# Grid attention on tokens ordered by column, with 192 or 256 keys per query tile, and weight splits one unit further ahead

## The reference

```python
def neighbourhood_attn(q, k, v, rpb):
    B, S = q.shape[0], q.shape[1]
    rows = S // GRID_W
    kr = min(NB_ROWS_MAX, rows)
    kc = NB_COLS
    ...
    row_start = jnp.clip(jnp.arange(rows) - kr // 2, 0, rows - kr)
    c_idx = jnp.arange(GRID_W)
    col_start = jnp.clip(c_idx - kc // 2, 0, GRID_W - kc)
    col_nb = col_start[:, None] + jnp.arange(kc)[None, :]
    ...
        s = jnp.einsum('bwhd,brwchd->bhwrc', q_row, k_nb,
                       preferred_element_type=jnp.float32) * scale + bias
        p = jax.nn.softmax(s.reshape(B, B_HEADS, GRID_W, kr * kc), axis=-1)
        p = p.reshape(B, B_HEADS, GRID_W, kr, kc).astype(v_nb.dtype)
        return jnp.einsum('bhwrc,brwchd->bwhd', p, v_nb)
```

```python
        mixed = jnp.einsum('bse,ed->bsd', jnp.concatenate([tok, mem_out], axis=-1), w_out[i])
        x = x + rms_norm(mixed, norm_mix_post[i])
        h = rms_norm(x, norm_ffn_pre[i])
        gu = jnp.einsum('bsd,df->bsf', h, w_gu[i])
        f = jnp.einsum('bsf,fd->bsd', jax.nn.silu(gu[..., :D_FF]) * gu[..., D_FF:], w_down[i])
        x = x + rms_norm(f, norm_ffn_post[i])
```

## Time and profile before

| | |
|---|---|
| runs | 2116.99, 2123.36, 2128.32 us, median 2123.36 |
| profiled execution | 2113.97 us, its span 2112.2 us, TensorE clock granted 0.978 |
| busy | PE 95%, weight loads of PE 77%, DVE 46%, ACT 37%, POOL 8% |
| chain that ended last | PE 89%, ACT 4%, DVE 4%, DMA 2%, issue 1% |
| DMA | 184.44 MB, 87 GB/s in the mean; a 512 KB weight load lands 3.2 to 3.3 us after its issue in the median |

### The profile page before, as it was taken

One profiled execution on the slowest core, in us unless ns is written; L12 is line 12 of the kernel. 1 busy time (PEld: TensorE's weight loads), 2 busy tenths in 40 slices (PEclk: granted clock), 3 DMA queues, 4 the chain that ended last, 5 costly groups with the idle time before them and its releaser, 6 DMA issues.

```text
span 2112.2 us, 24708 instructions
## 1 busy us (share of the span) xinstructions
PE 2013.9 (95%) x10206; PEld 1633.1 (77%) x10206; DVE 970.7 (46%) x1507; ACT 774.5 (37%) x1355; POOL 179.0 (8%) x201
## 2 busy tenths in 40 slices
PE   8899999999999998999999999979899999999997
PEld 6776778888878866778888878957777888888886
DVE  4465554443244286454443235252254455524632
ACT  4376432223232286432223223263363343312221
POOL 3010210000004040120000002000010010000000
PEclk9999999999999999999999999989899999999999
DMA  6620223233324220223223323201102332322232
GB/s 175 157 81 22 74 95 98 92 100 92 100 67 145 90 71 11 70 90 100 92 98 94 101 85 115 90 26 60 48 1 83 103 107 90 100 99 92 98 100 80
DMA packets 53448, 184.44 MB, mean 87 GB/s; under 512 B 6893, under 2 KB 8301, under 8 KB 53209
## 3 DMA queue, kind: packets, MB, share of 16 engines
q1 hardware_dynamic: 49656, 169.17, 24.5%
q0 software_dynamic: 3536, 13.64, 3.2%
q10 hardware_dynamic: 144, 0.06, 0.0%
HBM read 177.60 MB, written 5.24 MB: 87 GB/s over the span
## 4 chain that ended last, share of the span: by engine, by line
PE 89%; ACT 4%; DVE 4%; DMA 2%; issue 1%; POOL 0%; DVEq 0%; SPq 0%; ACTq 0%
PE bank L1162 25%; PE bank L1163 24%; PE bank L1164 24%; PE bank L1267 2%; PE bank L1282 2%; PE bank L1248 2%; PE bank L1188 2%; PE bank L1187 2%; PE bank L1186 2%; DMA w_raw<-in_w_mem_k 1%; DVE prob_short L883 1%; PE bank L1389 1%; PE bank L1422 1%; DVE prob_short L905 1%; ACT pt_short L585 1%
## 5 line engine op out<-in xcount | busy, mean ns | idle before, releaser
L1162 PE MATMUL bank<-h_hi,w_hi 128*128 128x512 f32 x1568 | 624.5, 398 | 40.8 <-DVE w_lo L794 19.9
L794 DVE TENSOR_TENSOR w_lo<-w_raw,w_hi 128x1024 fp32r<-128x1024 f32 (+1 forms) x326 | 404.3, 1242 | 508.7 <-ACT w_hi L491 508.2
L1163 PE MATMUL bank<-h_lo,w_hi 128*128 128x512 f32 x1568 | 617.1, 394 | 0.0
L1164 PE MATMUL bank<-h_hi,w_lo 128*128 128x512 f32 x1568 | 616.8, 393 | 0.0
L491 ACT CAST w_hi<-w_raw 128x1024 fp32r<-128x1024 f32 (+1 forms) x326 | 328.4, 1009 | 365.1 <-DMA w_raw<-in_w_down 77.7
L1162 PEld LDWEIGHTS bank<-h_hi,w_hi 128*128 128x128 f32 x1568 | 298.7, 191 | 114.7 <-issue 37.5
L1163 PEld LDWEIGHTS bank<-h_lo,w_hi 128*128 128x128 f32 x1568 | 299.1, 191 | 63.2 <-issue 1.9
L1164 PEld LDWEIGHTS bank<-h_hi,w_lo 128*128 128x128 f32 x1568 | 298.5, 190 | 63.4
L1162 PE MATMUL bank<-a_hi,w_hi 128*128 128x512 f32 (+1 forms) x752 | 290.5, 386 | 0.9 <-issue 0.9
L1164 PE MATMUL bank<-a_hi,w_lo 128*128 128x512 f32 (+1 forms) x752 | 289.2, 385 | 0.0
L1163 PE MATMUL bank<-a_lo,w_hi 128*128 128x512 f32 (+1 forms) x752 | 289.1, 384 | 0.0
(11 more groups left out here) (178 smaller groups left out, 1878.3 us busy)
## 6 DMA issues: line engine op xcount, KB each, us to landing
w_raw<-in_w_gu SPq DMA_DIRECT2D x88, 512.0 KB, 3.2
w_raw<-in_w_mlp_in SPq DMA_DIRECT2D x32, 512.0 KB, 3.2
w_raw<-in_w_mlp_out SPq DMA_DIRECT2D x32, 512.0 KB, 3.8
w_raw<-in_w_down SPq DMA_DIRECT2D x32, 448.0 KB, 3.3
w_raw<-in_w_out SPq DMA_DIRECT2D x24, 512.0 KB, 3.3
w_raw<-in_w_down SPq DMA_DIRECT2D x16, 512.0 KB, 3.5
w_raw<-in_w_gates SPq DMA_DIRECT2D x16, 512.0 KB, 3.2
w_raw<-in_w_qk_b SPq DMA_DIRECT2D x14, 512.0 KB, 3.3
```

The source lines that it names most:

```text
L794: nc.vector.tensor_tensor(slot(w_lo, v), slot(w_raw, v), slot(w_hi, v).bitcast(F32), ALU.subtract).then_inc(w_split, 1)
L1162: mm(acc, w1, hi, start=start, stop=False)
L1163: mm(acc, w1, lo, start=False, stop=False)
L1164: last = mm(acc, w2, hi, start=False, stop=end)
```

## The change

1. At the turn from layer 0 to layer 1, h is written in another order of tokens: by column of the grid, then row (column 0's 8 tokens, column 1's, and so on). Source and squares follow (by_column, columns_of). All of layer 1's projections and its attention are then in that order; the outputs are put back into the old order as they are copied out of PSUM, for memory heads too. A tile of 128 queries is then 16 whole columns, and its keys are 24, 32, 32 or 24 neighbouring columns: 192, 256, 256 and 192 keys, from key 0, 64, 192 and 320 on. Each step has two blocks of transposes and values a head in place of four.
2. So that key blocks fall on whole tiles of values, values are stored shifted by 64 tokens: each tile is read as two halves of 64 partitions (read_shifted_values).
3. The biases are one table of 128 by 256 a head (2 loads a pair) and a constant of masks (grid_masks, 128 by 640), loaded once by POOL before the phase; three additions a head (192, 192 and 256 columns) make the three tables.
4. Splits go one unit further: hi_to and lo_to to u + 3 in dense and values, to unit 7 at the start, to the eighth unit in leads and behind add_normed.

```diff
             for c in range(6):
-                for i in range(4):
-                    b0 = (6 - 2 * i) * GRID
-                    both = [dict(q=q_buf[rows(half), c, P * i:P * i + P], k=k_buf[rows(half), c, :],
-                                 bias=bias_grid[:, 2 * (c % 2) + half, b0:b0 + S], width=S, keys=S,
+                for i, (k0, keys, b0, blocks, tiles, key_rows) in enumerate(spans):
+                    both = [dict(q=q_buf[rows(half), c, P * i:P * i + P], k=k_buf[rows(half), c, k0:k0 + keys],
+                                 bias=bias_grid[:, 2 * (c % 2) + half, b0:b0 + keys], width=keys, keys=keys,
                                  first_key=0, sink=None, at=0) for half in range(2)]
...
-                hi_to(split + 3)
+                hi_to(split + 4)
...
-                        nc.scalar.copy(o_hi[:, steps[d].pair, :], ps[6 + steps[d].pair_no % 2][:, :]).then_inc(o_hi_done, 1)
+                        dst, src = o_hi[:, steps[d].pair, :], ps[6 + steps[d].pair_no % 2][:, :]
+                        if phase == 1:
+                            dst, src = by_column(dst), columns_of(src)
+                        nc.scalar.copy(dst, src).then_inc(o_hi_done, 1)
...
-            hi_to(6)
+            hi_to(7)
...
+            def read_shifted_values(g, accs):
+                for kt in range(4):
+                    for half in range(2):
+                        tile, to = (kt + half, 1 - half) if 0 < kt + half < 4 else (0, half)
+                        nc.scalar.activation(v_buf[rows(to), tile, 256 * g:256 * g + 256], accs[kt][rows(half), :256],
+                                             ACT.Copy, scale=col[rows(half), kt:kt + 1]).then_inc(acc_read_act, 1)
...
-                        lo_to(u + 2)
+                        lo_to(u + 3)
...
-                    trail(c, xT[:, c, :], h_hi[:, c, :], h_lo[:, c, :], pre)
+                    src, dst_hi, dst_lo = xT[:, c, :], h_hi[:, c, :], h_lo[:, c, :]
+                    if columns_first:
+                        src, dst_hi, dst_lo = by_column(src), columns_of(dst_hi), columns_of(dst_lo)
+                    trail(c, src, dst_hi, dst_lo, pre)
```

127 lines of the change are left out of this document (74 added, 53 removed).

## The result

The changed kernel took 2113.62 us, the median of six runs (2110.09 to 2115.30), beside 2124.47 for the kernel before. The ratio is 0.995 with a 95% interval of 0.9932 to 0.9969, so it is faster by 7 to 14 us. The forecast was 2100 us with a range of 2083 to 2112: direction right, gain of the medians 10.9 us where 23.2 were forecast, and the time just above the range. The profiled execution took 2111.95 us, its span 2110.2; against the profiled one of before that is only 2.0 us of span, and part of the story is why the two profiles say 2 and the medians 11.

What follows compares the result with a forecast made beforehand. The prediction took TensorE (PE) to bound the kernel: its work plus its gaps. Terms -26.1 + 0.7 + 1.6 + 5.6 - 12.0 + 5.6 + 1.4 gave -23.2 us, forecasting a 2100 us median, range 2083 to 2112.

Steps and rivals of the forecast that it cites:

- the one of the values: Layer 1's values before grid attention: reads in halves of 64 partitions lengthen PE's wait, +1.6 us.
- the reads just keep up: 0: Other stages: a unit takes 5.4 us, landing, cast and split 5.5, so splitting further ahead costs 0.
- So 9.1 against 13.45, six pairs: -26.1: Layer 1's grid attention: each head pair takes 9.1 us in place of 13.45, -26.1 us over six pairs.
- The passage: Grid attention: ScalarE's copy and VectorE's subtraction of a head pair, in series on the path, slower by 0.7 us through permuted access.
- the 0.3 for GpSimd's additions: Grid attention: GpSimd's table additions and VectorE's scaling stand in each other's way, 0.3 us a pair.
- the clock falling in the layer turn: Rival, turn of the layers: PE's pauses halve its clock, 1.2 us over the pace in six chunks, 2107 us; chance 0.05.
- So each of eight chunks gives its +0.7 to PE: +5.6: Turn from layer 0 to 1: permuted h_hi and h_lo writes lengthen each chunk by 0.7 us, +5.6 us.
- Four reads took 1.57 us, eight take 3.1: +1.6: Layer 1's values: the last group's reads before grid attention double in number and time, +1.6 us.
- PE goes on near 80.5: +5.6: Start: the memory's statistic waits behind unit 11's late cast, and the bias table copy starts later, +5.6 us.
- Both gaps go: 3.7 + 1.6 + 3.7 + 3.0, -12.0: gate_up, both layers: splitting the eighth unit ahead of the statistic removes PE's stops and the half clock after them, -12.0 us.
- +1.4: Before the window attention: the last read of memory values stands behind a later weight cast, +1.4 us.
- It lies 9.4 below the median: The profiled execution of before, 2113.97 us, against the timed median 2123.36; so 2090.8 became a forecast median of 2100.

Runs made afterwards that it cites:

- no_permute: The changed kernel with copies between the two token orders made in plain order, leaving out the reordering: 2098.02 us, 0.9901 of the kernel before.
- leads_only: The changed kernel with splits one unit further only where a stage is entered, two ahead elsewhere and at the start: 2101.63 us, 0.9917 of the kernel before.
- splits_only: The kernel before with only the splits moved one unit further: 2118.02 us, 1.0002 of the kernel before.
- late_sub: leads_only with VectorE's subtraction for a head pair's low half one step later: 2080.14 us, 0.9823 of the kernel before.
- best2: leads_only plus the late subtraction, the residual's next addition ahead of h_lo and idle matmuls in PE's pauses, table copy in one piece: 2063.99 us, 0.973.
- start_six: The changed kernel with units split only up to 6 at the start: PE goes on at 80.85 us, window attention entered at 125.74 us.

## Why the prediction was wrong, step by step

In the forecast's own terms the step that failed most is the one of the values: PE's wait ahead of the grid attention was priced at +1.6 and the clock behind it at nothing. The wait was 4.01 us for 1.66, the clock fell to half behind it, and grid attention and w_out together came out 3.9 to 5.5 us over the forecast. The second is "the reads just keep up: 0", which cost 3.7 us.

- **"So 9.1 against 13.45, six pairs: -26.1."** Right in its size, 9.08 at full speed, but in part by luck. The passage had 0.81 and not 0.7; the narrow pair without it took 8.27 and not 8.06 (no_permute); and the 0.3 for GpSimd's additions isn't there, since the pair from 796.74 to 805.82, in which GpSimd adds nothing, takes 9.08 as well. The three errors cancel. (Two pairs in 26.97 us are 13.49 each, a difference of 0.2 in the sum.) The attention still lost 3.3 us of its gain and w_out 2.2, by half speed. The forecast had the clock falling in the layer turn, as a rival with 0.05; there the later pauses were 1.2 and 1.6 us and the clock held.
- **"In other stages a unit takes 5.4 us [...] so the reads just keep up: 0."** Wrong: in the gates some units take 1.4 or 2.7 us, and PE waits 1.8 us for a_lo; +3.7. leads_only takes it back whole. Without half speed behind it, in splits_only, it is 2.7. The forecast looked at the mean stage and not at the shortest unit.
- **"So each of eight chunks gives its +0.7 to PE: +5.6."** Mechanism right, size 7.6: h_hi +0.5 and h_lo +0.37 in place of 0.3 and 0.4, in seven periods and in the first pause (5.32 for 4.52).
- **"Four reads took 1.57 us, eight take 3.1: +1.6."** Measured 3.92 and +2.35. Half the partitions is not half the price, nor the same price: 0.49 for 0.39. And the clock behind the longer wait was left out: half speed for up to 12 us of the attention from there, 3.8 us of time when the wait is filled (late_sub against best2).
- **"PE goes on near 80.5: +5.6."** Casts and copy as forecast; 6.7, and 1.2 more through half speed behind the wait. Of its two causes the later copy was worth only 0.7 (start_six).
- **"Both gaps go: 3.7 + 1.6 + 3.7 + 3.0, -12.0."** Right: -5.2 and -6.1.
- **"+1.4" ahead of the window attention.** Right: 1.42.
- **"It lies 9.4 below the median."** The forecast took its own profiled execution as any other and shifted the result. The second one, 11.65 us longer, shows that 9.7 us of that are one attention's half speed, 75.5 or 85.2 us for the same instructions. The shift was harmless for the median, but 6.7 us of the difference between the two profiles, in attentions that the change doesn't touch, mean nothing.

In medians the miss is 13.6 us, 1.1 of it because three more runs raised the median of before. By the stretches it is 2.7 to 3.7 (gates), 2.3 (start), 2.0 and 0.75 (turn, values), 0.7 (gate_up) and 3.9 to 5.5 in the grid attention and w_out, 12 to 15 in all; single traces don't divide it more finely. The range left this out since each unknown was bounded by itself: nearly all terms erred to the same side, and two places, the gates and the clock behind longer waits, were held to be free of charge.

## What to carry to other kernels

Splitting further ahead pays where PE enters a stage and costs where an in-order engine has its reads behind a cast that waits for a load; give it at the entry alone, and look for the shortest unit and the busiest stretch of DMA before making it a rule for all. When an engine's work is cut and short serial passages come onto the path, first look whether the passage can stand one step later: here that step was worth 15 to 21 us, more than the whole change. When a wait gets longer, price the clock behind it too: here it cost more than the wait's growth of 2.35 us. And compare two executions of one kernel, stretch by stretch, before an attention's few microseconds are explained.

## What the hardware showed that was not expected

- The stick-breaking attention takes 75.5, 80.0, 81.7 or 85.1 us with the same instructions, by how long PE stays at half speed around and after its first pause (clock 0.91 to 0.82 over the stretch); a row of idle matmuls in the pause made it 74.3 to 76.2 in four kernels.
- Half speed after a pause of 4.5 to 5.3 us cost 0 to 0.7 us where PE follows another engine's chunks, and 3.8 us behind a wait of 4.0 us ahead of the grid attention's steps.
- A read of 64 partitions by 256 columns on ScalarE takes 0.49 us, one of 128 by 256 takes 0.39.
- 3 MB from 12 partitions take 46 us, 0.5 MB from two 27 to 39 us, and 3 MB within HBM 16 us.
